# Weight rounding, product steps and a split slot moved around six waits of TensorE in a two-block transformer kernel

## The chip, the cores and the metric

The kernel runs on one core of a Trainium2 chip. A core has TensorE (PE, the matmuls), VectorE (DVE), ScalarE (ACT), GpSimd (POOL), SyncE (SP, which here only issues DMAs), an on-chip memory SBUF of 128 partitions, and 8 PSUM banks into which TensorE writes. Each engine runs its own list of instructions in order; the lists meet at semaphores. The metric is the device time of one execution in microseconds, the median over several; lower is better.

## What is computed

Two transformer blocks, one behind the other, on 512 tokens of width 1024, in fp32:

```python
x = x + token_mixer(rmsnorm(x, norm_mix), w_in, ...)        # HGRN2 scan and mLSTM, both directions
x = x + cross_attention(rmsnorm(x, norm_xattn), rmsnorm(mem, norm_mem), w_xq, w_xkv, w_xo)
x = x + squared_relu_mlp(rmsnorm(x, norm_mlp), w_up, w_down)
x = rmsnorm(x, norm_final)
# second block
proj = rmsnorm_2(x, norm_mix_2) @ w_in_2                    # splits into attention q, k, v; GLA q, k, v, gates
aq, ak = partial_rope(aq, positions), partial_rope(ak, positions)
y_att = windowed_gqa(aq, ak, av, sink) @ w_branch_attn
y_gla = gla_branch(...) @ w_branch_gla                      # chunked gated linear attention, both directions
x = x + (sigmoid(g_att) * y_att + sigmoid(g_gla) * y_gla) @ w_out
x = x + expert_choice_ffn(rmsnorm_2(x, norm_ffn), ...)      # 16 experts, 200 MB of weights
x = rmsnorm_2(x + sigmoid(rmsnorm_2(x, norm_ple) @ w_ple_gate) * (p @ w_ple), norm_final_2)
```

## The kernel before

**Products in three passes.** A weight matrix goes through as panels of 512 columns, and a panel as four parts of 256 rows by 512 columns. SP loads a part raw into one of four raw buffers (`raw_full`); part p is loaded once part p-4 is split. A part is then split into a rounded half "hi" and a remainder "lo" (`w_split` counts finished parts), and TensorE multiplies hi·hi, hi·lo, lo·hi. Who rounds differs from stage to stage. In `split_parts_of` GpSimd does both (L677 hi, L678 lo). In `split_hi`/`split_lo` ScalarE rounds (L687, signals `w_hi`) and GpSimd subtracts (L696, waits for `w_hi`). The table `HI` numbers the parts that ScalarE rounds, in their order.

**Slots.** A split part lies in a slot until TensorE is through with it. The first two slots are in `shared`, a third and a fourth in `spare`. `wide` lists the parts that may use four slots, `between` those that may use three; all others have two and alternate. `slot_free` makes whoever rounds wait for the part that was in the slot before.

**Steps.** `product_steps` is a generator. One step is the matmuls of one part for one of its four output groups (6 for 128x512), so a part takes 4 steps and a panel 16. Where a stage has small dependent matmuls (the scans, the attention), TensorE interleaves them with steps of the next product: `run_steps(steps, n)`. The order is thus written out by hand; no scheduler changes it.

**Banks.** Each use of a PSUM bank has a number in the table `STAGES`. TensorE waits for a bank to be free (`bank_claim`), whoever reads it waits for it to be full (`bank_take`).

**The stages that matter here**, in the order of the program:

- *Start.* ScalarE squares the four token tiles of x (L398) and takes the root (L401); VectorE inverts and scales (L410, L411); TensorE transposes each tile (L423); ScalarE and VectorE evacuate the eight transposed banks as hi (L730) and lo (L736); GpSimd splits the first two parts of the first product.
- *HGRN scan* (`hg_pe`, `hg_act`, `hg_pool`, `hg_dve`), eight chunks m, beside the product `proj_m` of 64 steps. `hg_evacuate` (L865) empties finished banks of `proj_m`. `keys` is a transpose (L837) that ScalarE copies out (L925).
- *Memory norm* (`mix_pe`). After the last 14 steps of `proj_m` TensorE transposes the 256 memory rows, 8 banks of 2 transposes each (`turn_pe`, L591), into the four LEFT banks, twice around. ScalarE frees the first four (conv_silu, L1178). The second four are freed by VectorE (L736, norm_mem). In VectorE's list the four instructions `gate_b(0)` to `gate_b(3)` (L1318) stand directly ahead of these evacuations; `gate_b(j)` reads the bank of the output group 12+j of `proj_m`, which steps 60 to 63 (the last four) complete.
- *Projections of the second block.* `proj_a` is a panel of 512 columns (below: a0 to a3, its parts), and then one of 288 columns (k, v and the GLA gates' inputs; below: kvz0 to kvz3). `proj_g` follows (g0 to g7), of which TensorE runs 8 steps (g0, g1). It then waits for the semaphore `roped`: VectorE has copied the banks out of PSUM (L2805, L2806) and turned queries and keys by 12 small tensor_tensor instructions (L2814 to L2819, once for queries, once for keys) and 2 copies (L2822). Then come the transposes L2351 and the attention, with the other steps of `proj_g` and `proj_v` in between. GpSimd meanwhile splits on: g0 to g3, a small one (L2255), g4 to g7.
- *GLA scan* (`gla_pe`), eight chunks, beside the product `proj_r`; behind it 14 steps, a transpose (`gla_turn(pe, 0)`, L1893), the rest, the first steps of `ygla`, `gla_turn(pe, 1)`. VectorE's L1881 makes what `gla_turn` reads.

## Time and profile before

| | |
|---|---|
| median of 3 runs (lowest to highest) | 1906.01 us (1905.35 to 1907.42) |
| profiled execution, device time | 1904.93 us |
| its span on the core | 1903.2 us |
| mean granted TensorE clock | 0.998 of full speed |
| busy: PE / ACT / DVE / POOL | 97% / 29% / 43% / 52% |

The span is the time from the first to the last recorded instruction. Busy shares are averages over all stages. TensorE is idle for 47.9 us of the span (1903.2 - 1855.3), in some forty waits, none over 8.5 us; the rows below hold those around the change. A row of the timeline gives the start, the duration from the start of the first to the end of the last instruction merged into it, engine, source line, operation, and in brackets how long the engine was idle before it and what ended that.

### The profile page before, as it was taken

To read this page: it belongs to the slowest core of one execution; us is meant where nothing else is said; L and a number is where in the kernel's file an instruction comes from. 1 tells how busy PE (TensorE), PEld (TensorE's weight loads), DVE (VectorE), ACT (ScalarE), POOL (GpSimd) and SP (SyncE) were. 2 spreads that over 40 slices of the span, in tenths; PEclk is the share of its full clock that TensorE was granted. 3 is DMA by queue.
4 is the path that set the end of the run, shared out by engine and by line. 5 is a ranking of instruction groups with operands and counts; after the bars stand their busy time and mean duration, and the time that the engine had idled before them with its cause. 6 is when DMAs were issued, how large, how long until landed. Compare 5 with 4: busy or idle time off the path is not lost.

```text
span 1903.2 us, 23463 instructions
## 1 busy us (share of the span) xinstructions
PE 1855.3 (97%) x9508; PEld 1376.5 (72%) x9508; DVE 816.5 (43%) x1219; ACT 560.7 (29%) x1129; POOL 989.3 (52%) x566
## 2 busy tenths in 40 slices
PE   7999999999999999999999999999999999999998
PEld 6888888788888888888777888888854444433446
DVE  4366677744523402322567476545241222211234
ACT  5535558342422201211223443342231000000025
POOL 6597867667378877887565796527600000000021
PEclk9999999999999999999999999999999999999999
DMA  6221124323133333333322333113999999999991
GB/s 208 83 78 45 45 68 160 95 67 100 36 98 89 100 100 91 98 100 100 104 88 67 89 89 88 56 36 131 355 379 402 427 428 427 427 427 428 422 372 57
DMA packets 82923, 335.89 MB, mean 176 GB/s; under 512 B 6528, under 2 KB 8320, under 8 KB 67712
## 3 DMA queue, kind: packets, MB, share of 16 engines
q1 hardware_dynamic: 79296, 322.47, 45.9%
q10 hardware_dynamic: 3520, 11.93, 1.7%
q8 instruction: 76, 1.25, 0.3%
q14 instruction: 31, 0.25, 0.0%
HBM read 328.08 MB, written 6.29 MB: 176 GB/s over the span
## 4 chain that ended last, share of the span: by engine, by line
PE 84%; DVE 7%; DMA 5%; ACT 2%; issue 1%; POOL 0%; SPq 0%; ACTq 0%; DVEq 0%; POOLq 0%
PE bank L638 54%; PE bank L2015 13%; DMA arena<-in_w_exp_up 3%; PE bank L2052 3%; PE bank L833 2%; DMA shared<-in_w_exp_up 2%; PE bank L2034 2%; PE bank L659 1%; PE bank L1740 1%; PE bank L1131 1%; PE bank L1739 1%; DVE arena L1881 1%; PE bank L1145 1%; PE bank L1583 1%; DVE bank L1189 1%
## 5 line engine op out<-in xcount | busy, mean ns | idle before, releaser
L638 PE MATMUL bank<-shared_r 128*128 128x512 f32 (+2 forms) x3180 | 728.8, 385 | 5.0 <-POOL shared_r L678 2.2
L638 PEld LDWEIGHTS bank<-shared_r 128*128 128x128 f32 x3180 | 575.4, 188 | 122.2 <-POOL shared_r L678 5.3
L677 POOL TENSOR_TENSOR shared_r<-shared,small 128x1024 fp32r<-128x1024 f32 (+1 forms) x151 | 292.2, 1935 | 291.2 <-PE bank L638 282.4
L678 POOL TENSOR_TENSOR shared_r<-shared,shared_r 128x1024 fp32r<-128x1024 f32 (+1 forms) x151 | 369.8, 2449 | 11.8
L677 POOL TENSOR_TENSOR spare_r<-arena,small 128x1024 fp32r<-128x1024 f32 x2 | 3.8, 1898 | 470.7 <-DMA arena<-in_w_ple_gate 470.7
L2015 PE MATMUL bank<-arena 128*64 128x512 f32 x624 | 185.0, 593 | 1.8 <-DMA arena<-in_w_exp_up 1.3
L2015 PE MATMUL bank<-shared,arena 128*64 128x512 f32 x592 | 179.6, 598 | 7.0 <-DMA shared<-in_w_exp_up 5.3
L638 PE MATMUL bank<-shared_r,arena_r 128*128 128x512 f32 x768 | 174.4, 389 | 0.0
L638 PEld LDWEIGHTS bank<-shared_r,arena_r 128*128 128x128 f32 x768 | 144.1, 188 | 29.9
L2015 PEld LDWEIGHTS bank<-shared,arena 128*64 128x64 f32 x592 | 57.9, 138 | 90.9 <-issue 90.9
L2015 PEld LDWEIGHTS bank<-arena 128*64 128x64 f32 x624 | 59.5, 137 | 57.8 <-issue 55.6
L2153 DVE TENSOR_TENSOR rows<-bank,rows 128x512 f32<-128x512 f32 x16 | 17.0, 1064 | 192.8 <-PE bank L2015 191.1
L638 PE MATMUL bank<-shared_r,spare_r 128*128 128x512 f32 (+1 forms) x384 | 86.5, 378 | 0.2 <-POOL spare_r L696 0.2
L2550 ACT ACTIVATE arena<-arena 128x512 f32<-128x512 f32 x32 | 20.2, 633 | 218.0 <-DVE arena L2781 217.6
L696 POOL TENSOR_TENSOR shared_r<-shared,shared_r 128x1024 fp32r<-128x1024 f32 x26 | 65.1, 2506 | 35.8 <-ACT shared_r L687 28.7
L638 PE MATMUL bank<-spare_r,shared_r 128*128 128x512 f32 x324 | 79.8, 399 | 2.8 <-DVE shared_r L736 1.1
L638 PEld LDWEIGHTS bank<-shared_r,spare_r 128*128 128x128 f32 x384 | 68.6, 188 | 13.4 <-POOL spare_r L696 0.4
L638 PEld LDWEIGHTS bank<-spare_r,shared_r 128*128 128x128 f32 x324 | 60.1, 188 | 17.6 <-issue 5.6
L524 DVE SCALAR_TENSOR_TENSOR X<-bank,small,X 128x512 f32<-128x512 f32 x16 | 11.9, 745 | 140.8 <-PE bank L638 140.8
L2781 DVE TENSOR_SCALAR arena<-bank 128x512 f32<-128x512 f32 x32 | 21.9, 685 | 104.3 <-PE bank L638 103.9
L638 PE MATMUL bank<-arena_r,shared_r 128*128 128x512 f32 x288 | 66.0, 389 | 0.3 <-DVE arena_r L736 0.3
L638 PEld LDWEIGHTS bank<-arena_r,shared_r 128*128 128x128 f32 x288 | 54.0, 188 | 11.7 <-issue 0.6
(462 smaller groups left out, 2648.1 us busy)
## 6 DMA issues: line engine op xcount, KB each, us to landing
shared<-in_w_in SPq DMA_DIRECT2D x80, 512.0 KB, 3.6
shared<-in_w_exp_up SPq DMA_DIRECT2D x11, 2048.0 KB, 26.6
arena<-in_w_exp_down SPq DMA_DIRECT2D x11, 2048.0 KB, 31.9
arena<-in_w_exp_gate SPq DMA_DIRECT2D x10, 2048.0 KB, 32.5
shared<-in_w_exp_gate SPq DMA_DIRECT2D x9, 2048.0 KB, 21.1
arena<-in_w_exp_up SPq DMA_DIRECT2D x9, 2048.0 KB, 24.0
shared<-in_w_up SPq DMA_DIRECT2D x32, 512.0 KB, 3.7
shared<-in_w_down SPq DMA_DIRECT2D x32, 512.0 KB, 3.6
```

The costliest lines, as they stand in the source:

```text
L638: ins = pe.matmul(dst, W_, x_, start=first, stop=final)
L659: ins = pe.matmul(bank[:, :], x[b][:, k, j * P:(j + 1) * P], halves[a][:, kk, :], start=k == 0 and (a, b) == (0, 0), stop=k == KT - 1 and ...
L677: link(pool.tensor_tensor(hi, raw(p), small[:, 18:19].to_broadcast([P, hi.shape[1]]), ALU.add))
L678: pool.tensor_tensor(lo, raw(p), hi.bitcast(F32), ALU.subtract).then_inc(S_("w_split"), 1)
L696: pool.tensor_tensor(lo, raw(p), hi.bitcast(F32), ALU.subtract).then_inc(S_("w_split"), 1)
L833: ins = pe.matmul(bank[keys, h * 64 + queries.start:h * 64 + queries.stop], HKL[g % 4][:, h, keys], HQL[g % 4][:, h, queries], start=True, ...
L1131: bank_ready(pe.matmul(bank[:, :], COUT[:, 4 + h, s * P:(s + 1) * P], COUT[:, h, :], start=True, stop=True), n)
L2015: ins = pe.matmul(banks_[h][x_rows(e), :], stay, panel[:, at, h * 512:(h + 1) * 512], start=k == 0, stop=k == KT - 1)
L2034: ins = pe.matmul(bank[:, :], OHT[i % 2][:, j * P:(j + 1) * P], YPS[b][:, h * 512:(h + 1) * 512], start=b == 0, stop=b == 1)
L2052: ins = pe.matmul(bank[:, dd * P:(dd + 1) * P], XS[:, j, d * P:(d + 1) * P], OH[:, j].rearrange("p e c -> p (e c)"), start=j == 0, stop=j ...
L2550: link(act.activation(HR[:, f % 4, :], HR[:, f % 4, :], ACT.Square))
L2781: bank_release(dve.tensor_scalar(HR[:, f % 4, :], bank[:, :], 0.0, None, ALU.max), n)
```

## The change

Six edits:

1. ScalarE takes over the rounding of the first part of `proj_h`, after a reordering of its squares and roots (the third root comes ahead of the fourth square); GpSimd keeps that part's subtraction.
2. In the HGRN scan ScalarE empties finished banks of `proj_m` also ahead of the copy of `keys`.
3. At the memory norm TensorE runs 13 steps, transposes 4 of 8 columns, runs the 14th step, and transposes the other 4.
4. ScalarE rounds a2 and a3 of `proj_a`.
5. kvz0 to kvz3 and all parts of `proj_g` have three split slots in place of two.
6. In the GLA scan one step each is put behind the `state` matmuls of chunks 5 and 6; behind the scan 13 steps are run ahead of the transpose in place of 14.

```diff
-    between = [p for w in range(PB["proj_m"] + 3, PB["out1"]) for p in panels[w]["parts"]]
+    between = [p for a, b in ((PB["proj_m"] + 3, PB["out1"]), (PB["proj_a"] + 1, PB["proj_v"])) for w in range(a, b) for p in panels[w]["parts"]]
...
+        square(0)
+        square(1)
+        root(0)
+        square(2)
+        root(1)
+        root(2)
+        square(3)
+        root(3)
+        split_hi(act, "proj_h", [0], 1)
         act.wait_ge(S_("cols_in"), 16)
...
-    HI = {}
-    for name, first in (("proj_h", 2), ("proj_m", 0), ("xk", 2), ("xv", 0), ("ple_gate", 2)):
+    HI = {panels[PB["proj_h"]]["parts"][0]: 1}
+    for name, first in (("proj_h", 2), ("proj_m", 0), ("xk", 2), ("xv", 0), ("proj_a", 2), ("ple_gate", 2)):
...
             if i < ST - 1:
+                hg_evacuate(act, done, hg_first + hg_each * m + 3)
                 n = hg_bank["keys", m, 0]
...
+        run_steps(steps, 4 * 16 - (hg_first + hg_each * 2 * ST) - 1)
+        pe.wait_ge(S_("mem_xs"), 1)
+        turn_pe(pe, MEMX, MT_, BASE["norm_mem"], range(4))
         for _ in steps:
             pass
-        pe.wait_ge(S_("mem_xs"), 1)
-        turn_pe(pe, MEMX, MT_, BASE["norm_mem"])
+        turn_pe(pe, MEMX, MT_, BASE["norm_mem"], range(4, KT))
...
+            if what == "state" and k + 1 < len(gla_order) and gla_order[k + 1][1] == 2 * ST - 1:
+                run_steps(steps, 1)
...
-        early("proj_h")
+        split_lo(pool, link, "proj_h", [0], 1)
+        split_parts_of(pool, link, "proj_h", count=1, skip=1)
...
-        rest("proj_a", 0)
+        split_parts_of(pool, link, "proj_a", count=2)
+        split_lo(pool, link, "proj_a", [2], 4)
+        split_parts_of(pool, link, "proj_a", skip=4)
...
-        run_steps(steps, 14)
+        run_steps(steps, 13)
...
         final_mix_act(act, BASE["down1"])
+        split_hi(act, "proj_a", [2], 4)
         act.dma_start(UPW[:, :, :], A["z_up"].rearrange("p (d s) -> p d s", d=2)).then_inc(S_("up_in"), 16)
```

Three places in the engines' lists. First ScalarE at the start, before (L398 the squares, L401 the roots, L730 the hi evacuations, L687 rounding):

```order
L398 ACTIVATE arena,small<-X 128x1024 x2
L401 ACTIVATE small<-small 128x1
L398 ACTIVATE arena,small<-X 128x1024
L401 ACTIVATE small<-small 128x1
L398 ACTIVATE arena,small<-X 128x1024
L401 ACTIVATE small<-small 128x1 x2
L730 ACTIVATE shared_r<-bank,PT 128x512 x8
L687 ACTIVATE spare_r<-shared 128x1024 x2
```

and now (the same functions at L395, L399, L740, L697):

```order
L395 ACTIVATE arena,small<-X 128x1024 x2
L399 ACTIVATE small<-small 128x1
L395 ACTIVATE arena,small<-X 128x1024
L399 ACTIVATE small<-small 128x1 x2
L395 ACTIVATE arena,small<-X 128x1024
L399 ACTIVATE small<-small 128x1
L697 ACTIVATE shared_r<-shared 128x1024
L740 ACTIVATE shared_r<-bank,PT 128x512 x8
L697 ACTIVATE spare_r<-shared 128x1024 x2
```

One rounding stands between the last root and the first evacuation.

Second TensorE at the memory norm, before (L638 product steps of `proj_m`, then of `xk` with 256 columns; L591 the transposes of the memory rows):

```order
L638 MATMUL bank<-spare_r,shared_r 128x512 x12
L638 MATMUL bank<-shared_r 128x512 x48
L638 MATMUL bank<-spare_r,shared_r 128x512 x24
L591 MATMUL bank<-ident,arena 128x128 x16
L638 MATMUL bank<-shared_r 128x256 x48
```

and now (L648 the product, L601 the transposes):

```order
L648 MATMUL bank<-spare_r,shared_r 128x512 x12
L648 MATMUL bank<-shared_r 128x512 x48
L648 MATMUL bank<-spare_r,shared_r 128x512 x18
L601 MATMUL bank<-ident,arena 128x128 x8
L648 MATMUL bank<-spare_r,shared_r 128x512 x6
L601 MATMUL bank<-ident,arena 128x128 x8
L648 MATMUL bank<-shared_r 128x256 x48
```

The last step of `proj_m`, the one that completes output group 15, has moved behind the first half of the transposes. VectorE's list is the same in both kernels.

Third GpSimd at `proj_g`, with what each instruction waits for: the parts g0 to g3 and the small split, before:

```order
L677 TENSOR_TENSOR shared_r<-shared,small 128x1024 [waits part_used,raw_full0]
L678 TENSOR_TENSOR shared_r<-shared,shared_r 128x1024 [waits pool_own]
L677 TENSOR_TENSOR shared_r<-shared,small 128x1024 [waits bank_full7,raw_full1]
L678 TENSOR_TENSOR shared_r<-shared,shared_r 128x1024 [waits pool_own]
L677 TENSOR_TENSOR shared_r<-shared,small 128x1024 [waits part_used,raw_full2]
L678 TENSOR_TENSOR shared_r<-shared,shared_r 128x1024 [waits pool_own]
L677 TENSOR_TENSOR shared_r<-shared,small 128x1024 [waits part_used,raw_full3]
L678 TENSOR_TENSOR shared_r<-shared,shared_r 128x1024 [waits pool_own]
L2255 TENSOR_TENSOR arena_r<-arena,arena_r 32x1024 [waits w_split,up_hi]
```

and now:

```order
L687 TENSOR_TENSOR shared_r<-shared,small 128x1024 [waits part_used,raw_full0]
L688 TENSOR_TENSOR shared_r<-shared,shared_r 128x1024 [waits pool_own]
L687 TENSOR_TENSOR shared_r<-shared,small 128x1024 [waits part_used,raw_full1]
L688 TENSOR_TENSOR shared_r<-shared,shared_r 128x1024 [waits pool_own]
L687 TENSOR_TENSOR spare_r<-shared,small 128x1024 [waits bank_full7,raw_full2]
L688 TENSOR_TENSOR spare_r<-shared,spare_r 128x1024 [waits pool_own]
L687 TENSOR_TENSOR shared_r<-shared,small 128x1024 [waits part_used,raw_full3]
L688 TENSOR_TENSOR shared_r<-shared,shared_r 128x1024 [waits pool_own]
L2273 TENSOR_TENSOR arena_r<-arena,arena_r 32x1024 [waits w_split,up_hi]
```

`bank_full7` is the signal that TensorE has completed kvz3. It stood at g1 and stands at g2: each part waits for the part three ahead of it instead of two (g0 for kvz1, g1 for kvz2, g2 for kvz3, g3 for g0).

## Rows read from the trace of the kernel before

**Rows 1.** The page, busy time and chain of work that ended last.

```profile
PE 1855.3 (97%) x9508; PEld 1376.5 (72%) x9508; DVE 816.5 (43%) x1219; ACT 560.7 (29%) x1129; POOL 989.3 (52%) x566
PE 84%; DVE 7%; DMA 5%; ACT 2%; issue 1%; POOL 0%; SPq 0%; ACTq 0%; DVEq 0%; POOLq 0%
```

**Rows 2.** TensorE's waits: who waited for whom, us in total, times, longest.

```profile
PE bank L423 <- DVE arena L411: 8.5, 2, 8.1
```

**Rows 3.** Timeline 0 to 32 us: start, us, engine, line, operation [idle <-releaser].

```profile
9.47 0.46 ACT L401 ACTIVATE small<-small 128x1 f32<-128x1 f32 x2
21.82 1.06 ACT L687 ACTIVATE shared_r<-shared 128x1024 fp32r<-128x1024 f32 x1 [1.66 <-DMA shared<-in_w_in]
10.18 2.31 POOL L677 TENSOR_TENSOR shared_r<-shared,small 128x1024 fp32r<-128x1024 f32 x1 [8.36 <-DMA shared<-in_w_in]
9.98 0.75 DVE L411 TENSOR_SCALAR arena<-X,small 128x1024 f32<-128x1024 f32 x1
10.85 2.19 DVE L411 TENSOR_SCALAR arena<-X,small 128x1024 f32<-128x1024 f32 x1
15.99 11.16 PE L638 MATMUL bank<-shared_r 128*128 128x512 f32 x48 [1.81 <-DVE shared_r L736]
```

**Rows 4.** Timeline of ScalarE and TensorE, HGRN chunk 2.

```profile
181.15 0.60 ACT L925 ACTIVATE arena<-bank 128x512 f32<-128x512 f32 x1 [3.45 <-PE bank L837]
182.25 1.26 ACT L865 ACTIVATE X<-bank,PT 128x512 f32<-128x512 f32 x2
182.99 1.66 PE L638 MATMUL bank<-shared_r 128*128 128x512 f32 x6 [1.03 <-ACT X L865]
```

**Rows 5.** Timeline of VectorE and TensorE at the memory norm.

```profile
298.64 2.48 DVE L1318 TENSOR_TENSOR arena<-bank,rows 128x512 f32<-128x512 f32 x4
301.28 3.22 DVE L736 SCALAR_TENSOR_TENSOR shared_r<-bank,PT,shared_r 128x256 fp32r<-128x256 f32 x8 [0.15 <-ACT shared_r L730]
299.33 1.81 PE L591 MATMUL bank<-ident,arena 128*128 128x128 f32 x8 [0.26 <-ACT arena L1178]
301.81 1.61 PE L591 MATMUL bank<-ident,arena 128*128 128x128 f32 x8 [0.67 <-DVE shared_r L736]
```

**Rows 6.** Timeline of GpSimd and TensorE at proj_a, kvz and proj_g.

```profile
929.50 3.24 POOL L678 TENSOR_TENSOR shared_r<-shared,shared_r 128x1024 fp32r<-128x1024 f32 x1
932.80 23.97 PE L638 MATMUL bank<-shared_r 128*128 128x512 f32 x144 [0.85 <-POOL shared_r L678]
958.11 11.18 PE L638 MATMUL bank<-shared_r 128*128 128x512 f32 x48 [1.33 <-POOL shared_r L678]
```

**Rows 7.** Timeline of VectorE's rope, and GpSimd and TensorE beside it.

```profile
958.26 2.11 DVE L2815 TENSOR_TENSOR arena<-arena,rows 128x256 f32<-128x256 f32 x1
960.29 2.62 DVE L2816 TENSOR_TENSOR arena<-arena,rows 128x256 f32<-128x256 f32 x1
962.84 0.41 DVE L2817 TENSOR_TENSOR arena<-arena,rows 128x256 f32<-128x256 f32 x1
966.02 2.41 DVE L2816 TENSOR_TENSOR arena<-arena,rows 128x64 f32<-128x64 f32 x1
958.01 2.08 POOL L677 TENSOR_TENSOR shared_r<-shared,small 128x1024 fp32r<-128x1024 f32 x1
960.17 2.46 POOL L678 TENSOR_TENSOR shared_r<-shared,shared_r 128x1024 fp32r<-128x1024 f32 x1
963.99 1.89 POOL L677 TENSOR_TENSOR shared_r<-shared,small 128x1024 fp32r<-128x1024 f32 x1 [1.36 <-PE bank L638]
969.82 2.84 PE L2351 MATMUL bank<-ident,arena 128*128 128x128 f32 x24 [0.53 <-DVE arena L2822]
```

**Rows 8.** Timeline of TensorE and VectorE at the end of the GLA scan.

```profile
1258.17 0.67 PE L1739 MATMUL bank<-arena 128*128 128x256 f32 x2 [1.06 <-DVE arena L1868]
1286.11 10.32 DVE L1881 SCALAR_TENSOR_TENSOR arena<-arena,rows 128x256 f32<-128x256 f32 x8 [1.26 <-ACTq L1823]
1296.49 1.97 PE L1893 MATMUL bank<-ident,arena 128*128 128x128 f32 x16 [0.20 <-DVE arena L1881]
```

More of the change, by code:

```diff
@@ L391, in first_act, with square, root @@
     def first_act(act):
+        def square(j):
+            act.wait_ge(S_("x_in%d" % j), 16)
+            act.activation(XS[:, j, :], X[:, j, :], ACT.Square, scale=1.0 / 32.0, accum_out=mean8[:, 0, 0, j:j + 1]).then_inc(S_("first_sq"), 1)
+        def root(j):
+            act.wait_ge(S_("first_sq"), j + 1)
+            act.activation(var[:, 0, j:j + 1], mean8[:, 0, 0, j:j + 1], ACT.Sqrt, bias=eps_).then_inc(S_("first_sd"), 1)
         act.wait_ge(S_("consts"), 1)
         act.activation(small[:, 19:20], eps_, ACT.Sqrt)
-        for j in range(ST + 1):
-            if j < ST:
-                act.wait_ge(S_("x_in%d" % j), 16)
-                act.activation(XS[:, j, :], X[:, j, :], ACT.Square, scale=1.0 / 32.0, accum_out=mean8[:, 0, 0, j:j + 1]).then_inc(S_("first_sq"), 1)
-            if j:
-                act.wait_ge(S_("first_sq"), j)
-                act.activation(var[:, 0, j - 1:j], mean8[:, 0, 0, j - 1:j], ACT.Sqrt, bias=eps_).then_inc(S_("first_sd"), 1)
+        square(0)
[7 more added lines that the diff above has]
+        split_hi(act, "proj_h", [0], 1)
         act.wait_ge(S_("cols_in"), 16)
@@ L584, in final_mix_dve, with turn_pe @@
         last.then_inc(S_("x_final"), 1)
-    def turn_pe(pe, src, n, base):
-        for d in range(KT):
+    def turn_pe(pe, src, n, base, columns=range(KT)):
+        for d in columns:
             bank = bank_claim(pe, base + d)
@@ L701, in next_stage @@
         return min([w for w in PB.values() if w > PB[name]] + [len(panels)])
-    HI = {}
-    for name, first in (("proj_h", 2), ("proj_m", 0), ("xk", 2), ("xv", 0), ("ple_gate", 2)):
-        for p in [p for w in range(PB[name], next_stage(name)) for p in panels[w]["parts"]][first:1 if name == "xv" else None]:
+    HI = {panels[PB["proj_h"]]["parts"][0]: 1}
+    for name, first in (("proj_h", 2), ("proj_m", 0), ("xk", 2), ("xv", 0), ("proj_a", 2), ("ple_gate", 2)):
+        for p in [p for w in range(PB[name], next_stage(name)) for p in panels[w]["parts"]][first:{"xv": 1, "proj_a": 4}.get(name)]:
             HI[p] = len(HI) + 1
```

## The prediction, as put on record before the changed kernel ran

> **What bounds the kernel now.** I read the busy table and the chain of waits first, then TensorE's waits, then the timeline around each wait that the diff touches. TensorE is busy 97% of the span and holds 84% of the chain [rows 1]. Its largest wait, 8.1 us, is the start, until the first scaled tile of x is there [rows 2]; the rest are waits of about 1 us. So a gain can only come from TensorE's idle time, 47.9 us in all, and a microsecond anywhere ahead of the experts moves everything behind it, since the expert weights' DMAs are released by TensorE's progress too. Against that, VectorE and GpSimd are idle about half the time on average, but at some places it is one of them that ends TensorE's wait, and there the order in their own lists decides.
>
> **Edit 1, start.** VectorE scales the fourth tile in 2.19 us, from 10.85 to 13.04, although GpSimd began its rounding at 10.18 and the scaling ended about half a microsecond after that rounding did (12.49) [rows 3]. The tile before took 0.75, ahead of it [rows 3]. With ScalarE rounding, GpSimd stands idle at 10 us. The last root now follows the fourth square, ends at about 10.1 instead of 9.93 [rows 3], so the scaling starts at 10.5 and ends at 11.25: 1.8 us earlier. Everything from there to TensorE's first product (13.04 to 15.99, 2.95 us) stays: 14.2. ScalarE's rounding takes 1.06 [rows 3], from about 10.2 (the weights have landed by 10.18) to 11.25, just ahead of the first transposed bank; GpSimd's subtraction, 2.46 by the like row [rows 7], then ends at 13.8, in time. Part 1 is ready at about 18.2 and needed at 14.2 + 5.6 = 19.8 (half of 11.16, [rows 3]). I take -1.8; bounds -2.2 (root and scaling both earlier) and 0 (the subtraction comes late: then the first product waits for it instead of for VectorE).
>
> **Edit 2, banks.** ScalarE sits idle 3.45 us before the copy L925, then does other work and two evacuations, and TensorE waits 1.03 for the first of these [rows 4]. Both banks were full before that idle time, so both evacuations (1.26) fit into it, the wait goes, and the rounding behind them comes 1.26 earlier, and with it GpSimd. I take -1.1; bounds -1.4 and 0 (the scan's chain over three engines takes it back).
>
> **Edit 3, memory norm.** The held-back step is 6 matmuls, 6 x 0.2325 = 1.4 us (11.16 / 48). It is meant for the waits of 0.26 and 0.67 [rows 5]. But it completes the bank that `gate_b(3)` reads, and `gate_b(3)` is the last of the four L1318 (298.64, 2.48), directly ahead of the eight evacuations L736 (301.28, 3.22, 0.40 each) that free the banks for the second half of the transposes [rows 5]. Now: TensorE reaches the first half 1.4 earlier but ScalarE still frees its banks from 299.3 on, so that half ends at 301.0 as before. The step follows, complete at 302.5; `gate_b(3)` until 303.15 (2.48 / 4); the evacuations free banks at 303.6, 304.0, 304.4, 304.8; the last transposes end at 305.3 instead of 301.81 + 1.61 = 303.4 [rows 5], and the next product starts behind them. VectorE makes up a little behind it, where it waited for GpSimd. I take +1.8; bounds -0.93 (both waits filled, nothing lost) and +2.2.
>
> **Edit 4, a2 and a3.** TensorE waits 0.85 for a2: it ended a1 at 931.95, and GpSimd's subtraction ended at 929.50 + 3.24 = 932.74 [rows 6]. The slot of a0 is free at 926.5; ScalarE rounds until 927.7, GpSimd subtracts until about 930.9. The 0.85 goes. ScalarE's later DMAs (z_up, x_keep) wait 2.6 us for a3's slot; nothing needs them before 960.
>
> **Edit 5, third slot.** The wait of 1.33 for g0 [rows 6]: g0 no longer waits for kvz2 but for kvz1. All times below are on the old clock with edit 4 in it. TensorE takes a2 and a3 from 931.95, kvz0 at 942.9, and (23.97 - 10.9) / 4 = 3.27 per part [rows 6], so it ends kvz1 at 949.4, kvz3 at 956.0, and g0 follows at once, split at 954.1. So far -2.2. But after g0 and g1 (11.18, [rows 6]), at 967.1, TensorE needs `roped`, for which it already waited 0.53 [rows 7]. That is the step on which this forecast rests.
>
> The rope's 12 tensor_tensor instructions take 0.41 or less when GpSimd is idle (962.84), but 2.11 and 2.62 beside it: L2815 ends at 960.37, just behind GpSimd's end at 960.09, L2816 at 962.91, just behind 962.63, the small L2816 at 968.43 [rows 7]. One of them gets through for each instruction of GpSimd. What let the rope end by 969.8 was that GpSimd waited for slots: 1.36 us before 963.99, in which three instructions passed, and again behind 968.35, after which the last three and the copies took 1.4. With three slots GpSimd does not wait. g0 begins at 949.8 (kvz1 done, plus the 0.4 by which 963.99 followed the end of g0 in the kernel before), each part takes 2.08 + 0.08 + 2.46 beside a blocked VectorE [rows 7], and the slots of kvz3 (956.4) and g0 (961.9) are free when g2 (958.4) and g3 (962.9) are reached; the small split 967.6 to 970.0, g4 to 974.5, only then does it wait (g5 needs g2 done by TensorE). VectorE begins at 956.7, one instruction at each end: 958.7, 960.8, 963.3, 965.3, 967.9, 970.3 (six of queries), 972.2 (two, the second is 0.2), 974.7, and 1.4 for the rest: 976.1. Before: 969.8. So edits 4 and 5 together cost +6.3. Nothing behind takes it back: the attention runs on TensorE without long waits. Bounds: -2.7 (0.85 + 1.33 + 0.53, the rope wholly inside g0 and g1) and +8.7 (one more instruction of GpSimd, 2.4, gets in between).
>
> The Trainium skill's page "SBUF — State Buffer", section "Who interferes with whom", says that a VectorE instruction with two SBUF inputs contends with a GpSimd instruction that reads SBUF, and that the one issued second is blocked for the whole of the other. Rows 7 agree for 128 partitions. No row shows the small split of 32 partitions beside such an instruction; by the rule it blocks as well (+6.3), were it left out the sum would be about 2.4 smaller.
>
> **Edit 6, GLA.** The wait of 1.06 before `out` of the last chunk is filled by a step of 1.4: -1.06 on TensorE [rows 8]. But the second transpose waited 0.20 for L1881, whose 8 instructions took 10.32 beside GpSimd [rows 8], and the chain to it begins with the first transpose, which one more step ahead of it puts at +0.3. Most of the gain turns into a longer wait there; GpSimd's parts shift against VectorE, which may help or hurt. I take -0.3; bounds -1.06 and +1.0.
>
> **Sum.** -1.8 - 1.1 + 1.8 + 6.3 - 0.3 = +4.9. The profiled execution would go from 1904.93 to 1909.8; it lies 1.08 below the median of the runs, which would go from 1906.01 to 1910.9. A change of 0.2%, 3.8 us, is about what a measurement of this kernel can tell from none.
>
> **Rivals.**
> *The holes are filled as named.* For it: each edit moves work exactly into a wait that rows 4 to 8 show. Against it: at three of the six places the wait behind is on another engine's list. All of it: -1.8 - 1.1 - 0.93 - 0.85 - 1.33 - 1.06 = -7.1, 1898.9. 5%.
> *VectorE slips through.* The rope is not held up (GpSimd pauses at each semaphore long enough, or the loads of g2 and g3 come late and make pauses): edits 4 and 5 give -2.7, the sum is -4.1, 1901.9. For it: two of the small instructions passed between 965.88 and 966.02, at one boundary of GpSimd [rows 7]. Against: the rows of 2 us each. 13%.
> *Half starved.* Two or three instructions pass more than I count: +3, sum +1.6, 1907.6. 23%.
> *Memory norm harmless* (-0.93), rope as forecast: +2.2, 1908.2. 6%.
> *The starved rope*, the forecast, is the slower side; its place is `roped`, its price about 2.2 us for each instruction that no longer finds a pause, and it decides once `roped` comes later than 971.2: then it costs over 1.4, more than the other edits give together. 53%.
>
> **The numbers.** The likeliest is 1910.9. Faster by over 0.2%: the first two rivals, 0.18. Within 0.2%: the next two, 0.29. Slower: 0.53. The forecast's own range is 1908.5 to 1913.5 (up: one more instruction of GpSimd in the rope; down: edits 1, 3 and 6 each somewhat better than taken). The range for 8 in 10 reaches down to the second rival without holding its whole lower part: 1902.5 to 1914.
>
> **What would show it.** Right: TensorE's first product at 14.2; no wait for L865 in chunk 2; VectorE's fourth L1318 start after the held-back step, and the product with 256 columns about 1.9 later relative to the scan's end; no wait of TensorE for a2 or g0; GpSimd without pause from g0 to the small split; the rope's instructions at 2 us each, and a wait of 8 to 9 us before the transposes L2351 (now another line number) for VectorE's copies. Wrong: rope instructions at 0.4 us beside a busy GpSimd, or a wait there under 3 us; then the time falls to 1902 to 1906. If the first product starts later than 15 us, edit 1 gave its gain to GpSimd's subtraction.

## The result, and the profile of the changed kernel

| | before | changed |
|---|---|---|
| median, 7 runs each, side by side | 1906.01 us | 1912.47 us |
| lowest to highest | 1904.31 to 1907.53 | 1910.42 to 1913.89 |
| ratio of the two, 95% interval | | 1.0034 [1.0024, 1.0044] |
| profiled execution, its span, mean granted clock | 1904.93, 1903.2, 0.998 | 1911.8, 1910.0, 0.993 |

The change costs 6.5 us, 0.34%. The forecast was 1910.9 with a range of 1902.5 to 1914.0: the median is inside, and slower by over 0.2% was the likeliest of the three outcomes. The sum was right for partly wrong reasons, as the table shows. It gives where TensorE stands against the kernel before at the same place of the program (changed minus before, us), read from the two timelines:

| place | offset | term behind it: measured (forecast) |
|---|---|---|
| first product | -0.15 | edit 1: -0.15 (-1.8) |
| HGRN chunk 2 | -1.5 | edit 2: -1.4 (-1.1) |
| last product step before the memory norm's waits | -2.0 | the same edit, further chunks: -0.5 (0) |
| second product of the stage behind the memory norm | +1.9 | edit 3: +3.9 (+1.8) |
| first product of proj_a | +1.97 | |
| first matmul of the attention | +9.64 | edits 4 and 5: +7.7 (+6.3) |
| behind the GLA scan | +8.57 | edit 6: -1.07 (-0.3) |
| end of the span | +6.8 | the experts and the end: -1.8 (0) |

The page of the changed kernel, busy time and chain, beside [rows 1]:

```profile
PE 1859.0 (97%) x9508; PEld 1381.0 (72%) x9508; DVE 814.7 (43%) x1219; ACT 564.5 (30%) x1132; POOL 981.7 (51%) x563
PE 86%; DVE 5%; DMA 5%; ACT 1%; issue 1%; SPq 0%; POOL 0%; ACTq 0%; DVEq 0%
```

TensorE executes the same 9508 matmuls, yet is busy 3.7 us longer. That is the first sign that something other than waits has changed. Its largest waits, beside [rows 2]:

```profile
PE bank L2369 <- DVE arena L2841: 9.0, 1, 9.0
PE bank L433 <- DVE arena L421: 8.2, 1, 8.2
PE bank L2030 <- DMA shared<-in_w_exp_up: 4.9, 3, 2.7
PE bank L601 <- ACT arena L1191: 1.7, 1, 1.7
PE bank L601 <- DVE shared_r L746: 1.2, 1, 1.2
```

The wait for the rope was 0.5 us and is now the longest of the kernel. No wait for a GpSimd split of proj_a or g0 is left. (In the changed file the lines of before stand 10 to 19 further on: L601 are the memory rows' transposes, L1331 gate_b, L2369 the transposes of queries and keys.)

The start, timeline, beside [rows 3]:

```profile
10.32 0.75 DVE L421 TENSOR_SCALAR arena<-X,small 128x1024 f32<-128x1024 f32 x1
8.21 5.80 PE L433 MATMUL bank<-ident,arena 128*128 128x128 f32 x32 [8.21 <-DVE arena L421]
15.84 3.42 PE L648 MATMUL bank<-shared_r 128*128 128x512 f32 x14 [1.83 <-DVE shared_r L746]
```

VectorE's fourth scaling takes 0.75 us and ends at 11.07, 2 us earlier than before, even a little better than forecast. But the 32 transposes run without a pause until 14.0: TensorE itself had become the bound. It nearly was already in the kernel before, where the first 24 ended at 12.77, less than 0.3 us ahead of the fourth scaling's end at 13.04:

```profile
8.14 4.63 PE L423 MATMUL bank<-ident,arena 128*128 128x128 f32 x24 [8.14 <-DVE arena L411]
13.09 1.09 PE L423 MATMUL bank<-ident,arena 128*128 128x128 f32 x8 [0.32 <-DVE arena L411]
```

ScalarE and TensorE in HGRN chunk 2, beside [rows 4]:

```profile
177.34 1.24 ACT L875 ACTIVATE X<-bank,PT 128x512 f32<-128x512 f32 x2
180.88 0.60 ACT L936 ACTIVATE arena<-bank 128x512 f32<-128x512 f32 x1 [2.30 <-PE bank L847]
181.49 1.64 PE L648 MATMUL bank<-shared_r 128*128 128x512 f32 x6
```

Both evacuations now stand inside ScalarE's idle time, and TensorE's wait of 1.03 is gone.

The memory norm, beside [rows 5]:

```profile
297.33 1.82 PE L601 MATMUL bank<-ident,arena 128*128 128x128 f32 x8 [1.67 <-ACT arena L1191]
298.90 2.59 PE L648 MATMUL bank<-spare_r,shared_r 128*128 128x512 f32 x6
301.52 0.69 DVE L1331 TENSOR_TENSOR arena<-bank,rows 128x512 f32<-128x512 f32 x1 [3.00 <-PE bank L648]
302.13 3.52 DVE L746 SCALAR_TENSOR_TENSOR shared_r<-bank,PT,shared_r 128x256 fp32r<-128x256 f32 x8
302.66 1.97 PE L601 MATMUL bank<-ident,arena 128*128 128x128 f32 x8 [1.17 <-DVE shared_r L746]
304.28 6.81 PE L648 MATMUL bank<-shared_r 128*128 128x256 f32 x48
```

gate_b(3) waits 3.00 us for the held-back step, and the evacuations stand behind it, as forecast. But the step takes 2.59 us instead of 1.6, and the product 6.81 where it took about 6.0. The same stretch by windows (the third number from the end is the granted clock):

```profile
298.00:300.00 2.00, 1.90 (x9) 1.27 (x8) 0.53 (x1) 1.88 (x6) 2.00 (x2) 0.82 0.13 48
302.00:304.00 2.00, 1.34 (x7) 1.14 (x8) 1.89 (x6) 0.61 (x2) 0.91 (x1) 0.50 0.23 89
306.00:308.00 2.00, 2.00 (x18) 2.00 (x18) 1.97 (x2) 2.00 (x4) 1.83 (x1) 0.97 0.03 8
```

The granted clock is 0.50 (1.2 GHz) for some 7 us; in the kernel before it is 1.00 throughout this stretch. It fell at about 299.3, 2 us after a wait of 1.67 us had ended.

The rope, beside [rows 7]:

```profile
958.35 1.96 DVE L2833 TENSOR_TENSOR arena<-arena,rows 128x256 f32<-128x256 f32 x1
960.23 2.11 DVE L2834 TENSOR_TENSOR arena<-arena,rows 128x256 f32<-128x256 f32 x1
962.14 2.45 POOL L688 TENSOR_TENSOR spare_r<-shared,spare_r 128x1024 fp32r<-128x1024 f32 x1
962.27 2.61 DVE L2835 TENSOR_TENSOR arena<-arena,rows 128x256 f32<-128x256 f32 x1
969.29 2.33 POOL L2273 TENSOR_TENSOR arena_r<-arena,arena_r 32x1024 fp32r<-32x1024 f32 x1
969.36 2.56 DVE L2838 TENSOR_TENSOR arena<-arena 128x256 f32<-128x256 f32 x1
977.54 4.96 PE L2369 MATMUL bank<-ident,arena 128*128 128x128 f32 x24 [9.03 <-DVE arena L2841]
```

One VectorE instruction gets through for each of GpSimd's, eight times with 1.8 to 2.6 us each. The copies out of PSUM just ahead of them (L2824 and L2825, 955.23 to 958.2) keep their 0.26 and 0.41 us beside the same GpSimd work. The transposes then take 4.96 us instead of 2.84: the granted clock is 0.50 here too.

The end of the GLA scan, beside [rows 8]:

```profile
1295.51 9.24 DVE L1896 SCALAR_TENSOR_TENSOR arena<-arena,rows 128x256 f32<-128x256 f32 x8 [0.99 <-ACTq L1838]
1305.11 1.91 PE L1908 MATMUL bank<-ident,arena 128*128 128x128 f32 x16
```

The second transpose no longer waits for VectorE.

### The profile page after: what moved, and what is told of

Its sections match the earlier page's. It is cut to its first block, busy times and chain, and to the rows that moved or that the text cites. A ratio compares the mean times of both kernels' runs of the same rounds, so it can differ in the third digit from the quotient of the medians.

```text
span 1910.0 us, 23463 instructions
## 1 busy us (share of the span) xinstructions
PE 1859.0 (97%) x9508; PEld 1381.0 (72%) x9508; DVE 814.7 (43%) x1219; ACT 564.5 (30%) x1132; POOL 981.7 (51%) x563
## 4 chain that ended last, share of the span: by engine, by line
PE 86%; DVE 5%; DMA 5%; ACT 1%; issue 1%; SPq 0%; POOL 0%; ACTq 0%; DVEq 0%
PE bank L648 55%; PE bank L2030 13%; DMA arena<-in_w_exp_up 3%; PE bank L2067 3%; PE bank L843 2%; PE bank L2049 2%; DMA shared<-in_w_exp_up 2%; PE bank L669 1%; PE bank L2184 1%; PE bank L1753 1%; PE bank L1144 1%; PE bank L1752 1%; PE bank L1757 1%; PE bank L1158 1%; PE bank L1596 1%
## 5 line engine op out<-in xcount | busy, mean ns | idle before, releaser
L648 PE MATMUL bank<-shared_r 128*128 128x512 f32 (+2 forms) x3084 | 711.5, 387 | 1.8 <-DVE shared_r L746 1.8
L648 PEld LDWEIGHTS bank<-shared_r 128*128 128x128 f32 x3084 | 561.2, 188 | 115.8 <-issue 6.0
L687 POOL TENSOR_TENSOR shared_r<-shared,small 128x1024 fp32r<-128x1024 f32 (+1 forms) x144 | 279.6, 1941 | 259.4 <-PE bank L648 258.9
L688 POOL TENSOR_TENSOR shared_r<-shared,shared_r 128x1024 fp32r<-128x1024 f32 (+1 forms) x144 | 353.4, 2454 | 11.4
L687 POOL TENSOR_TENSOR spare_r<-arena,small 128x1024 fp32r<-128x1024 f32 x2 | 3.8, 1892 | 469.0 <-DMA arena<-in_w_ple_gate 469.0
L648 PE MATMUL bank<-shared_r,arena_r 128*128 128x512 f32 x768 | 174.4, 389 | 0.0
L648 PEld LDWEIGHTS bank<-shared_r,arena_r 128*128 128x128 f32 x768 | 144.1, 188 | 29.9
L706 POOL TENSOR_TENSOR shared_r<-shared,shared_r 128x1024 fp32r<-128x1024 f32 x29 | 73.1, 2523 | 60.9 <-ACT shared_r L697 53.7
L648 PE MATMUL bank<-shared_r,spare_r 128*128 128x512 f32 (+1 forms) x432 | 98.4, 381 | 0.2 <-POOL spare_r L706 0.2
L648 PE MATMUL bank<-spare_r,shared_r 128*128 128x512 f32 (+1 forms) x372 | 88.3, 390 | 2.8 <-DVE shared_r L746 1.1
L648 PEld LDWEIGHTS bank<-shared_r,spare_r 128*128 128x128 f32 x432 | 77.4, 188 | 16.3 <-issue 1.2
L648 PEld LDWEIGHTS bank<-spare_r,shared_r 128*128 128x128 f32 x372 | 67.0, 189 | 17.5 <-issue 5.6
L648 PE MATMUL bank<-arena_r,shared_r 128*128 128x512 f32 x288 | 66.2, 390 | 0.7 <-ACT arena L1836 0.4
L648 PEld LDWEIGHTS bank<-arena_r,shared_r 128*128 128x128 f32 x288 | 53.9, 188 | 12.5 <-issue 1.3
```

Of the source, the lines that this page charges most:

```text
L648: ins = pe.matmul(dst, W_, x_, start=first, stop=final)
L687: link(pool.tensor_tensor(hi, raw(p), small[:, 18:19].to_broadcast([P, hi.shape[1]]), ALU.add))
L688: pool.tensor_tensor(lo, raw(p), hi.bitcast(F32), ALU.subtract).then_inc(S_("w_split"), 1)
L706: pool.tensor_tensor(lo, raw(p), hi.bitcast(F32), ALU.subtract).then_inc(S_("w_split"), 1)
```

## Experiments

Each was timed against the kernel before on the same chip. A trace shows one execution; medians are over 5 to 11 runs. "us over before" is the difference of medians.

**The changed kernel again.**

> The changed kernel unchanged, on the chip of the three others. Theory (what edit 3 costs depends on whether the granted clock falls at the memory norm): if the first transposes of queries and keys again wait 9 us and take 5.0, the time is 6.0 to 6.8 us over the kernel before in the median; at the memory norm a granted clock of 0.5 in this execution or 1.00, in which case the products behind it start 2 us earlier. Rival (the first profile was an exception, the clock falls at neither place as a rule): under 5 us over the kernel before.

1911.64 us, 7.25 over before (ratio 1.0036 [1.0024, 1.0048]). Rope: wait 9.03, transposes 4.97; memory norm: granted clock 0.50 from about 299 to 305.6. The first profile was no exception at these two places. Behind the GLA scan it was: the offset of +8.06 there is +8.4 at the end of the span, and nothing is taken back. This is the base that the next runs are held against, by their distance from the kernel before.

**GpSimd made to pause.**

```diff
-        split_parts_of(pool, link, "proj_g", count=4)
+        split_parts_of(pool, link, "proj_g", count=2)
+        pool.wait_ge(S_("roped"), 1)
+        split_parts_of(pool, link, "proj_g", count=2, skip=2)
```

> The changed kernel, but GpSimd waits for the semaphore roped before it splits g2 (the third slot stays). Theory (the rope is starved because GpSimd never pauses): VectorE's rope instructions behind the end of g1's subtraction (about 962) take 0.4 us or less, roped comes at about 963 instead of 977.5, TensorE's wait before the transposes of queries and keys (9.0 us) is gone, its granted clock does not fall there, the transposes take 2.8 instead of 5.0, and the attention starts at about 972.5 instead of 983.4: minus 10.9, of which the waits for expert weights may take back up to 2, so 1901.6 to 1903.6 us. Rival (the third slot only moves the work, GpSimd's time is what is short): g2 and g3 come late and TensorE waits for them inside the attention, minus 5 or less: 1907 or more.

1900.69 us, 3.9 under before (ratio 0.998 [0.9971, 0.9989]) and 11.1 better than the changed kernel. VectorE's first rope instructions, GpSimd and TensorE:

```profile
956.36 1.97 DVE L2835 TENSOR_TENSOR arena<-arena,rows 128x256 f32<-128x256 f32 x1
958.25 0.41 DVE L2836 TENSOR_TENSOR arena<-arena,rows 128x256 f32<-128x256 f32 x1
962.07 1.89 POOL L687 TENSOR_TENSOR spare_r<-shared,small 128x1024 fp32r<-128x1024 f32 x1 [4.02 <-DVE arena L2843]
966.37 2.79 PE L2371 MATMUL bank<-ident,arena 128*128 128x128 f32 x24
```

The first instruction lies beside g1's subtraction (1.97 us), the rest take 0.43 or less. The rope is done 4.4 us before TensorE wants it, and GpSimd's 4.02 us of standing still cost nothing: TensorE does not wait for g2 or g3. From the start of kvz0 to the attention it is 27.67 us (942.64 to 970.31), in the changed kernel 38.81 (944.63 to 983.44): 11.14, as much as the medians differ by. (TensorE reaches kvz0 2.0 earlier too; the granted clock at the memory norm stayed at 1.00 in this execution.) The rope is starved by GpSimd's never pausing; the rival, that GpSimd's time is short, falls.

**Without edit 5.**

```diff
-    between = [p for a, b in ((PB["proj_m"] + 3, PB["out1"]), (PB["proj_a"] + 1, PB["proj_v"])) for w in range(a, b) for p in panels[w]["parts"]]
+    between = [p for w in range(PB["proj_m"] + 3, PB["out1"]) for p in panels[w]["parts"]]
```

> The changed kernel without edit 5: kvz and proj_g have two slots again, all else stays. Theory (starved rope plus a clock that falls in the 9 us wait): GpSimd's pauses come back, TensorE waits about 1.3 us for g0 and under 1 for roped, and the attention starts 7.7 to 8.5 us earlier than in the changed kernel: 1904.0 to 1905.5 us. Rival (edit 4 is part of it: two roundings on ScalarE move GpSimd against VectorE): only half comes back, 1908 or more.

1902.78 us, 1.8 under before (ratio 0.9992 [0.9983, 1.0001], not told apart from no change), 9.0 better than the changed kernel. GpSimd pauses again:

```profile
961.60 0.41 DVE L2836 TENSOR_TENSOR arena<-arena,rows 128x256 f32<-128x256 f32 x1
962.75 1.89 POOL L687 TENSOR_TENSOR shared_r<-shared,small 128x1024 fp32r<-128x1024 f32 x1 [1.36 <-PE bank L648]
```

TensorE waits 1.33 for g0 and 0.53 for the rope, as in the kernel before, and from proj_a's first product to the attention it takes 51.86 us against 53.01: edit 4 alone is worth about 1.1. Against the changed kernel's 60.68 for the same stretch that is 8.8, nearly the whole gain. The 7.7 that was expected at least is the cost of edits 4 and 5 together (the table); edit 4's own 1.1 comes on top.

**Edit 5 on the kernel before, without edit 4,** with 17 matmuls at the start (for those see below).

```diff
-    between = [p for w in range(PB["proj_m"] + 3, PB["out1"]) for p in panels[w]["parts"]]
+    between = [p for a, b in ((PB["proj_m"] + 3, PB["out1"]), (PB["proj_a"] + 1, PB["proj_v"])) for w in range(a, b) for p in panels[w]["parts"]]
...
+        keep_busy(pe, BASE["norm_mix"], 17)
```

> The kernel before with edit 5 alone (third slot for kvz and proj_g) and with the 17 matmuls at the start. At the start: VectorE's fourth scaling still ends at 13.0 beside GpSimd's rounding, so the first product starts at 16.0 as before or at most 0.2 earlier: the matmuls are worth nothing without edit 1. At the rope: by the starved-rope theory the third slot alone does all the harm: TensorE waits 8 to 9 us for roped with the clock at 0.5, attention 7 to 8 us later than in the kernel before, less 1 to 2 in the waits for expert weights: plus 6 us. Rival (edit 4's two roundings on ScalarE are needed for it): under plus 3 us.

1915.08 us, 10.2 over before (ratio 1.0051 [1.0039, 1.0064]). TensorE's transposes of queries and keys:

```profile
978.36 4.71 PE L2352 MATMUL bank<-ident,arena 128*128 128x128 f32 x24 [9.03 <-DVE arena L2823]
```

From proj_a's first product (922.10) to the attention (984.01) it is 61.91 us, 8.9 more than before: the third slot alone does the harm. The sum missed by 4 us. Of that 1.3 are there by proj_a (922.10 against 920.79): the clock fell near the start (0.50 from about 16.3 to 19.7 us), which had been put at nothing. Another 0.9 to 1.9 lie at the rope, and the profiled execution is the shortest of the five, 1.5 under their median.

**Without edit 3.**

```diff
-        run_steps(steps, 4 * 16 - (hg_first + hg_each * 2 * ST) - 1)
-        pe.wait_ge(S_("mem_xs"), 1)
-        turn_pe(pe, MEMX, MT_, BASE["norm_mem"], range(4))
         for _ in steps:
             pass
-        turn_pe(pe, MEMX, MT_, BASE["norm_mem"], range(4, KT))
+        pe.wait_ge(S_("mem_xs"), 1)
+        turn_pe(pe, MEMX, MT_, BASE["norm_mem"])
```

> The changed kernel without edit 3: all 14 steps of proj_m, then all eight columns of the memory rows. By the prediction (1.8 us lost to the held-back step that gate_b(3) waits for) it gains 1.8 us: 1910.7. By the traces of both kernels (the two waits of 1.7 and 1.2 us are followed by a granted clock of 0.5 for 7 us, so step, transposes and the next product are slow too) it gains 3.5 to 4, less what waits for expert weights take back: 1908.5 to 1909.5, with the granted clock at 1.00 from 290 to 310.

1909.25 us, 4.7 over before (ratio 1.0024 [1.0015, 1.0033]), 2.6 better than the changed kernel (1.0036 [1.0024, 1.0048]; the intervals overlap, so the traces carry the reading). Granted clock 1.00 from 290 to 310. The second half of the transposes:

```profile
299.72 1.61 PE L601 MATMUL bank<-ident,arena 128*128 128x128 f32 x8 [0.67 <-DVE shared_r L746]
```

In the kernel before they start at 301.81, which is 2.1 later by the offset of edits 1 and 2 alone. In an execution with edit 3 and the clock up (the kernel with the pause) they start at 301.89; where it fell, at 302.66 and 302.25, and the product behind them is slow too. These executions began up to 0.4 us apart, so I measure the stretch itself, from the first of the last `proj_m` steps that read `spare_r` (293.47 in the kernel before) to the second product behind the transposes (309.03 there). It takes 15.4 to 15.7 us in the six executions without edit 3, 17.4 in the three with edit 3 and the clock up, and 18.6 to 19.5 in the four where it fell. So edit 3 costs 1.8 with the clock up, the forecast, and 3.0 to 4.0 with it down; the median says 2.6. Of seven profiled executions with edit 3 and gate_b(3) ahead of the evacuations the clock fell in four, of the six without edit 3 in none.

**gate_b(3) behind the evacuations,** edit 3 kept.

```diff
-        for j in range(ST):
+        for j in range(ST - 1):
             gate_b(j)
         for d in range(KT):
             evac_lo(dve, BASE["norm_mem"] + d, MEMTS[1][:, d, :], MEMTS[0][:, d, :], par("norm_mem", d), MEM)
+        gate_b(ST - 1)
```

> The changed kernel with gate_b(3) moved in VectorE's list behind the eight evacuations of the memory norm; TensorE's order is kept. Theory (the held-back step hurts because gate_b(3) stands ahead of the evacuations that free the banks): VectorE's evacuations start at about 299 instead of 302.1, TensorE's second wait (1.2 us) goes, the second half of the transposes starts at 300.4 instead of 301.8 to 302.7, minus 1.4 where the clock stays up and up to 3.3 where it fell before. Rival (the step itself, put between, is what is late, or ScalarE's hi evacuations free the banks): minus 0.5 or less.

1909.95 us, 5.6 over before (ratio 1.0026 [1.0016, 1.0036]), 1.7 better than the changed kernel (these intervals overlap too).

```profile
298.94 1.66 DVE L746 SCALAR_TENSOR_TENSOR shared_r<-bank,PT,shared_r 128x256 fp32r<-128x256 f32 x4 [0.75 <-ACT shared_r L740]
300.03 1.07 PE L601 MATMUL bank<-ident,arena 128*128 128x128 f32 x8
302.52 0.68 DVE L1331 TENSOR_TENSOR arena<-bank,rows 128x512 f32<-128x512 f32 x1
```

The evacuations start at 298.94, the second half of the transposes at 300.03 without a wait, and the stretch measured above takes 15.6: it was gate_b(3)'s place. But against the kernel without edit 3 nothing is won (the product at 316.77 there and 316.79 here): by missing ahead of the first half the step lengthens the wait there from 0.23 to 1.36, about what it fills behind.

**TensorE kept busy through the rope wait.**

```diff
         run_steps(steps, rope_steps)
+        keep_busy(pe, BASE["turn_qk"], 76)
         pe.wait_ge(S_("roped"), 1)
```

> The changed kernel with 76 matmuls of the identity by itself on TensorE ahead of its wait for roped (about 8 us at the high clock if each takes 0.107). The rope stays starved and its end stays at 977.5. Theory (2.1 us of what edits 4 and 5 cost is TensorE's clock, which falls in the wait of 9 us): granted clock 1.00 through 985, the 24 transposes take 2.8 instead of 5.0, minus 2.1. Should each take twice as long (two passes), they run past the end of the rope and add about 7 us, and the transposes still take 2.8. Rival (the transposes are slow for another reason): they still take 5.0.

1918.04 us, 13.7 over before (ratio 1.0068 [1.0056, 1.0081]). Each such matmul counts twice (152 records), so they ran past the end of the rope, as the second case of the expectation had it:

```profile
966.87 17.13 PE L540 MATMUL bank<-ident 128*128 128x128 f32 x152
983.83 2.78 PE L2370 MATMUL bank<-ident,arena 128*128 128x128 f32 x24
```

Granted clock 1.00 from 955 to 990, transposes 2.78 instead of 4.97: of edits 4 and 5's cost 2.1 us is the clock. The kernel as a whole, 6.4 slower than the changed one, only shows that padding must be measured before it is counted.

**TensorE kept busy before the start,** with 36 and then with 17 matmuls of the identity by itself.

```diff
         pe.wait_ge(S_("ident"), 1)
+        keep_busy(pe, BASE["norm_mix"], 36)
         for j in range(ST):
```

> The changed kernel with 36 more matmuls of the identity by itself (128x128, results unused) on TensorE ahead of the first transposes, from about 2 us on. Theory (the transposes of the start run slowly because TensorE was idle before them, though the granted clock reads 1.00): with the added matmuls 32 transposes go at 0.11 us each, the last 8 end 0.9 behind the fourth scaling (11.07), at about 12.0 instead of 14.0, and the first product starts at about 13.9 instead of 15.84: minus 1.9, 1910.6 us. Rival (they are slow for another reason, the 400 GB/s of loads or VectorE and ScalarE beside them): their pace stays, product at 15.8, no change: 1912.5.

1914.61 us, 10.0 over before (ratio 1.0051 [1.0038, 1.0065]): the expected gain did not come. The 36 ran until 12.7 and delayed everything (product at 18.0), but the 32 transposes behind them took 3.66 instead of 5.80.

> The changed kernel with 17 matmuls of the identity by itself ahead of the first transposes (with 36 they ran until 12.7 us and came in the way, but the transposes behind them went at 0.11 us each instead of 0.18). They end at 7.7, ahead of the first scaled tile (8.2). Theory (TensorE's pace at the start depends on what it did before): the last 8 transposes end 0.9 behind the fourth scaling, at about 12.0, the first product starts at 13.9 instead of 15.84, minus 1.9: about 1909 to 1910 if the changed kernel is at 1911. Rival (the idle 0.5 us behind them or the pause between tiles slows them again): product at 15.5 or later, no change.

1910.74 us, 6.35 over before (ratio 1.003 [1.0019, 1.0042]), 0.9 better than the changed kernel (within the noise of the two medians). The trace is clearer. The fourth scaling, the last 24 transposes and the product, then two windows of 1 us (third number from the end: granted clock):

```profile
10.41 0.75 DVE L421 TENSOR_SCALAR arena<-X,small 128x1024 f32<-128x1024 f32 x1
9.49 2.84 PE L434 MATMUL bank<-ident,arena 128*128 128x128 f32 x24 [0.24 <-DVE arena L421]
14.14 8.24 PE L649 MATMUL bank<-shared_r 128*128 128x512 f32 x28 [1.81 <-DVE shared_r L747]
```

```profile
15.00:16.00 1.00, 1.00 (x5) 0.76 (x4) 1.00 (x3) 1.00 (x3) 0.92 (x2) 0.61 1.04 355
16.00:17.00 1.00, 1.00 (x4) 0.81 (x3) 1.00 (x2) 1.00 (x2) 1.00 (x1) 0.50 0.40 49
```

The product starts at 14.14, the 14.2 of the prediction. In the kernel before, with the same 17 matmuls but without edit 1 (edit 5 on the kernel before, above), the fourth scaling still took 2.19 and the product started at 16.12. So edit 1 and a TensorE that is up to pace are each worth next to nothing alone and 1.85 us together (15.99 to 14.14). And then the clock fell to 0.50 from about 15.2 to 18.6, after the idle 1.8 us between transposes and product, and took all of it back. From the first product to those steps that read `spare_r`, ahead of the memory norm, it is 277.2 us here and 275.5 to 275.7 in the eleven other executions with edits 1 and 2; the 1.42 by which the product leads that of the changed kernel's second run (15.56) are gone at 291 us (291.30 against 291.22). Where it fell in the kernel before with edit 5, the same stretch is 1.3 longer than in the kernel before.

**All that helped.** The changed kernel with the pause and without edit 3; then with the 17 matmuls too.

> The changed kernel with GpSimd waiting for roped ahead of g2, and without edit 3 (all steps of proj_m first). If the two effects add (10.4 us from the first alone; edit 3 costs 2.1 us with the granted clock up and 4 with it down): the kernel before minus 3.9 for the first, minus 2 to 3 more: ratio 0.9965 to 0.997, about 5.5 to 6.5 us under the kernel before. If the waits for expert weights take it back, 4 us under.

1897.69 us, 7.2 under before, ratio 0.9962 [0.9949, 0.9974]: the two effects add, and a little more than expected.

> The same with 17 matmuls of the identity by itself ahead of the first transposes. The product started 1.4 us earlier with them, but the granted clock was then 0.5 for 3 us and 0.6 us were left. Another 0.6 us under the same kernel without them; if the clock's fall takes all of it, none.

1896.15 us, 8.7 under before, ratio 0.9955 [0.9941, 0.9969]: the best kernel of this study, 16 us or 0.8% under the changed one in distance from before, and 1.5 under the former, where 0.6 or nothing was expected. Its product starts at 13.96, 1.36 ahead of the former's 15.32; in this execution the clock did not fall, and the lead is 1.5 at the memory norm.

**Without edit 6,** against the first of these two.

```diff
-            if what == "state" and k + 1 < len(gla_order) and gla_order[k + 1][1] == 2 * ST - 1:
-                run_steps(steps, 1)
...
-        run_steps(steps, 13)
+        run_steps(steps, 14)
```

> The first of these kernels without edit 6 (no steps behind the state matmuls of chunks 5 and 6, 14 steps ahead of the transpose). By the prediction edit 6 is worth 0.3 us, by the trace of the changed kernel 1.07 (from 9.64 to 8.57 us behind the kernel before across the end of the GLA scan): the wait of about 1.06 before the last chunk's out is back, and the time is 0.3 or 1.1 us over that kernel's. In the trace the eight VectorE instructions that the second transpose waits for take 10.3 us instead of 9.2 if GpSimd's phase against them is what differed.

1898.57 us (ratio to before 0.9967 [0.9954, 0.9979]), 0.9 over it, which the medians alone would not tell from nothing; by its trace 1.05 (the product behind the second transposes 1.63 later, of which 0.58 stem from before the attention). From the attention to that product it is 325.0 us in the three executions without edit 6 and 323.8 to 324.0 in the eleven with it. VectorE's eight instructions and GpSimd beside them, without edit 6:

```profile
1280.55 10.32 DVE L1892 SCALAR_TENSOR_TENSOR arena<-arena,rows 128x256 f32<-128x256 f32 x8 [1.29 <-ACTq L1834]
1285.44 2.21 POOL L687 TENSOR_TENSOR shared_r<-shared,small 128x1024 fp32r<-128x1024 f32 x1 [1.01 <-PE bank L648]
```

and with it:

```profile
1279.74 9.23 DVE L1894 SCALAR_TENSOR_TENSOR arena<-arena,rows 128x256 f32<-128x256 f32 x8 [0.99 <-ACTq L1836]
1284.22 1.93 POOL L687 TENSOR_TENSOR shared_r<-shared,small 128x1024 fp32r<-128x1024 f32 x1 [1.68 <-PE bank L648]
```

GpSimd pauses 1.68 instead of 1.01, and VectorE gets more done in the longer pause. That the pause is the cause is read from these rows; no run changed it by itself.

## Why the prediction was right or wrong

**Edit 1, -1.8, measured -0.15.** The step that failed is "everything from there to TensorE's first product (2.95 us) stays". The 2.95 held only because TensorE had caught up while VectorE was slow. The first 24 transposes took 4.63 us in the kernel before, 0.19 each, and ended less than 0.3 us ahead of the fourth scaling; once VectorE no longer held up the last eight, the transposes were the bound. Even the -0.15 is not clear of the scatter: in the nine executions with edit 1 and no added matmuls the product starts between 15.32 and 16.56, in the one of the kernel before at 15.99. The value lay inside the bounds (-2.2 to 0), whose upper end was given another reason, GpSimd's subtraction. That ended at 13.54, in time, so the sign named for it (a first product later than 15 us) came true for another cause.

**Edit 2, -1.1, measured -1.4** at chunk 2 and half a microsecond more by the end of the scan, for which no row had been weighed. Most of that 0.5 lies between 217 and 235 us, where two waits of TensorE for VectorE (0.21 and 0.15, L833) are gone. No run takes edit 2 out. But from the first product to the steps that read `spare_r` it is 277.5 us in the kernel before and 275.5 to 275.7 in every execution with edits 1 and 2 in which the clock did not fall near the start, so the -1.9 is no accident of one trace.

**Edit 3, +1.8, measured +3.9** in the first trace. The mechanism held in each step, and the size too: with the clock up edit 3 costs 1.8, and moving gate_b(3) frees the evacuations. The term that was missing is the clock, 1.2 to 2.1 more where it fell, 2.1 in the first trace.

**Edits 4 and 5, +6.3, measured +7.7.** Both waits went, and then the rope ended where it was put: forecast 6.3 later relative to the product before, measured 5.75 (7.72 minus the offset of 1.97). The small split did block an instruction (2.56 beside 2.33). The Trainium skill's page "SBUF — State Buffer", section "Who interferes with whom", states the rule without naming a number of partitions, and this row agrees for 32. The other 2.1 is again the clock, shown by the run that kept TensorE busy.

**Edit 6, -0.3, measured -1.07.** "Most of the gain turns into a longer wait there" failed. One step fewer stood between the first transposes and the last group of proj_r, so ScalarE's four copies came in one row, the chain started 0.26 earlier behind the transposes (5.34 to 5.08), and VectorE's instructions took 9.24 instead of 10.32 beside GpSimd's longer pause.

**Not in the sum: -1.8 behind the GLA scan.** There the weights' DMAs end TensorE's waits for shared buffers (6.7 us before, 4.9 now). It is tempting to say that a TensorE that arrives later waits less, but the other traces speak against it: the changed kernel's second execution arrives 8.1 later than the kernel before and loses another 0.3, and the kernel with the pause arrives 4.6 earlier and ends 4.7 earlier. Over the twelve other executions this last stretch is between 1.5 us shorter and 0.4 longer than in the kernel before, without regard to who arrives late. So the -1.8 is mostly what one execution differs from another by; what decides it stays open.

**The rivals.** "VectorE slips through" and "half starved" fell with the eight blocked instructions. Errors of +1.65, -0.8, +2.1, +1.4, -0.8 and -1.8 leave +1.9 in the sum (before rounding): the range held because they compensated, which is luck, and not because each term was known.

## What to carry to other kernels

A free buffer that lets one engine run without a pause can starve another that its instructions block: look for short VectorE instructions that end with GpSimd's, and give the pause back by a wait at the place where it costs nothing (here 11 us for one line). When a stall is removed, ask what ran during it: time it again at its own pace, not at the pace that it had behind the stall. Before a step is moved into a hole, list who reads what it completes and what stands behind that reader.

## What the runs showed of the hardware

**TensorE's clock fell after waits shorter than I had looked for.** In the profiled executions it fell at the memory norm after a wait of 1.4 to 1.7 us, in four of seven; the other three had waited 1.5 and kept 1.00, so the length of the wait does not tell them apart. Of the four executions with added matmuls at the start, it fell in two after the idle 1.8 us ahead of the first product (at 15.2 and 16.3 us) and kept 1.00 in two. It was back at 1.00 after 3 to 7 us. The price was 1.2 to 2.1 us at the memory norm and 1.3 to 1.5 near the start. What decides it between executions stays open.

**At the start the granted clock in the profile reads 1.00, and the pace says otherwise.** The changed kernel at the start, and at the rope's transposes with the clock at 0.50:

```profile
9.00:10.00 1.00, 1.00 (x7) 1.00 (x6) 0.96 (x3) 0.89 (x3) 0.00 (x0) 1.00 1.07 401
978.00:980.00 2.00, 2.00 (x12) 2.00 (x11) 0.00 (x0) 1.05 (x2) 0.00 (x0) 0.50 0.52 200
```

Six to seven transposes in a microsecond in both; with the 17 matmuls ahead of them it is 12 (10 to 11 us), beside the same loads. The Trainium skill's page "TensorE: Matmul & The Clock Gate", section "Part 1: The HAM clock gate", says that the engine's clock is at the lower of its two levels until it has been busy; the pace agrees with that, the profile's row of the granted clock does not.
